# Hybrid encoder block on one core: compressed rows from the first token-major pass, first attention's values as a fifth seven-product group

## The reference, cut to what matters

```
h = rmsnorm(x); proj = h @ w_in                      # columns: AQ AK AV AG | CQ CKV KR BG | MG
oa = diff_attention(aq, ak, av)                      # 8 heads; ya = (rmsnorm(oa) * silu(ag)) @ w_oa
q  = rmsnorm(cq)  @ w_uq;  kv = rmsnorm(ckv) @ w_ukv # cq and ckv: 512 compressed columns each
ob = attention(q_nope|rope(q_rope), k_nope|rope(kr), vb);  yb = (ob * silu(bg)) @ w_ob
x  = x + (sigmoid(ga) * ya + sigmoid(gb) * yb) @ w_out;  out = rmsnorm(x)
```

## Time and profile before

| | us |
|---|---|
| Median of 3 runs (1456.37 to 1456.82) | 1456.66 |
| Profiled execution, its own time | 1456.54 |
| Its span in the profile | 1454.7 |
| PE busy | 1438.2 (99% of the span) |
| DVE busy | 982.3 (68%) |
| ACT busy | 653.6 (45%) |
| DMA, mean rate | 143 GB/s |

### The profile page before, as it was taken

The page is one execution under the profiler, slowest core; times in us unless marked ns, Lnnn a source line. Parts: engine busy times, 40 slices in busy tenths (PEclk is TensorE's granted clock), DMA queues, the critical chain, the costliest instruction groups (busy, mean ns, idle before and its releaser), DMA issues.

```text
span 1454.7 us, 18138 instructions
## 1 busy us (share of the span) xinstructions
PE 1438.2 (99%) x6780; PEld 1198.1 (82%) x6780; DVE 982.3 (68%) x1354; ACT 653.6 (45%) x835; POOL 44.6 (3%) x58
## 2 busy tenths in 40 slices
PE   8999999999999999999999999999999999999997
PEld 7888888888888888888888888888888888888886
DVE  6967798888777666666665643666667353578966
ACT  7534353434345455454543335565565122324434
POOL 0000000000000111001110000000000000000000
PEclk9999999999999999999999999999999999999999
DMA  8349585757562322322222334322332444616674
GB/s 300 137 153 309 157 276 174 259 183 225 186 191 83 83 78 77 89 79 79 79 72 73 97 91 145 87 74 58 93 127 70 150 125 145 202 59 228 194 249 182
DMA packets 189535, 207.94 MB, mean 143 GB/s; under 512 B 19360, under 2 KB 144416, under 8 KB 188832
## 3 DMA queue, kind: packets, MB, share of 16 engines
q1 hardware_dynamic: 181952, 189.25, 42.3%
q10 hardware_dynamic: 7520, 17.83, 3.1%
HBM read 187.12 MB, written 19.92 MB: 142 GB/s over the span
## 4 chain that ended last, share of the span: by engine, by line
PE 91%; DVE 4%; DMA 2%; SPq 1%; issue 1%; ACT 1%; POOL 0%; POOLq 0%; DVEq 0%
PE duo L2028 28%; PE duo L2030 27%; PE duo L2029 27%; PE duo L2081 2%; PE duo L2055 1%; PE duo L2058 1%; DMA start_y<-start_columns 1%; DVE m_lo L1422 1%; PE duo L2114 1%; SPq L598 1%; PE duo L2108 1%; PE duo L2077 1%; PE duo L2073 0%; PE duo L2076 0%; PE duo L2074 0%
## 5 line engine op out<-in xcount | busy, mean ns | idle before, releaser
L1310 DVE TENSOR_TENSOR w_lo<-w_raw,w_hi 128x1024 fp32r<-128x1024 f32 (+1 forms) x134 | 157.4, 1175 | 157.8 <-ACT w_hi L756 157.2
L2028 PE MATMUL duo<-h_hi,w_hi 128*128 128x512 f32 x656 | 260.2, 397 | 0.0
L2030 PE MATMUL duo<-h_hi,w_lo 128*128 128x512 f32 x656 | 255.9, 390 | 0.0
L2029 PE MATMUL duo<-h_lo,w_hi 128*128 128x512 f32 x656 | 255.7, 390 | 0.0
L756 ACT ACTIVATE w_hi<-w_raw 128x1024 fp32r<-128x1024 f32 (+1 forms) x134 | 136.2, 1017 | 173.9 <-DMA w_raw<-in_w_ob_dram 65.3
L857 ACT ACTIVATE m_hi<-m_raw 128x2048 fp32r<-128x2048 f32 (+1 forms) x56 | 98.0, 1753 | 118.8 <-PE duo L2030 47.7
L2030 PEld LDWEIGHTS duo<-h_hi,w_lo 128*128 128x128 f32 x656 | 123.1, 188 | 26.7
L2028 PEld LDWEIGHTS duo<-h_hi,w_hi 128*128 128x128 f32 x656 | 123.3, 188 | 23.9 <-DVE q_hl L1315 0.3
L2029 PEld LDWEIGHTS duo<-h_lo,w_hi 128*128 128x128 f32 x656 | 123.4, 188 | 23.7
L1422 DVE TENSOR_TENSOR m_lo<-m_raw,m_hi 128x2048 fp32r<-128x2048 f32 (+3 forms) x61 | 121.2, 1989 | 21.3 <-ACT m_hi L857 20.8
L2028 PE MATMUL duo<-m_hi,h_hi 128*128 128x512 f32 x320 | 126.0, 394 | 2.0 <-DVE h_lo L1458 1.0
(11 more groups left out here) (296 smaller groups left out, 2807.6 us busy)
## 6 DMA issues: line engine op xcount, KB each, us to landing
m_raw<-in_w_in_dram SPq DMA_DIRECT2D x94, 512.0 KB, 4.6
w_raw<-in_w_in_dram SPq DMA_DIRECT2D x164, 256.0 KB, 3.2
o_raw<-in_w_out_dram SPq DMA_DIRECT2D x32, 512.0 KB, 5.5
w_raw<-in_w_oa_dram SPq DMA_DIRECT2D x32, 256.0 KB, 3.4
sig<-gates SPq DMA_DIRECT2D x8, 1024.0 KB, 6.5
w_raw<-in_w_ob_dram SPq DMA_DIRECT2D x32, 256.0 KB, 3.4
spare<-in_w_in_dram SPq DMA_DIRECT2D x13, 512.0 KB, 4.4
h_raw<-in_w_in_dram SPq DMA_DIRECT2D x13, 512.0 KB, 5.1
```

Source lines behind the costliest of these rows:

```text
L1310: dve.tensor_tensor(w_lo[:, piece.slot, 0:cols], w_raw[:, piece.slot, 0:cols], w_hi[:, piece.slot, 0:cols].bitcast(F32), ALU.subtract).the ...
L2028: pe.matmul(dst, lhs_hi, rhs_hi, start=start, stop=False)
L2029: pe.matmul(dst, lhs_hi, rhs_lo, start=False, stop=False)
L2030: return pe.matmul(dst, lhs_lo, rhs_hi, start=False, stop=stop)
```

## The change

The first pass now reads CQ and CKV, whose rows come out token-major. ACT squares each row with an accumulator and scales it by its inverse root, and the rows are stored to `compressed`. AV becomes group 0 of five seven-product groups; its blocks are stored to `values` without a sigmoid. In the compressed stage the 16 pieces for CKV and CQ are gone; SP loads the stored rows back as `c_tok`, PE turns them with 8 x 4 transposes (`turn_c`) within the half pieces 2 to 11, ACT and DVE split them straight from PSUM with the gain. The first BG pair comes first, then KR, then `token_values`, one token tile at a time in two banks, head 7's extras 8 to 11 between its tiles. `rope_angles` moves to step 2, `rope_tables` to step 3, `rotate` to step 5. Three orders are changed: DVE makes the low part first also in the step after each group's first step and in one more step of the `w_out` group, and the first quarter of the gated rows is split one step earlier. Cut to its core:

```diff
-A_STEPS, C_STEPS, B_STEPS = 6, 24, 4
+A_STEPS, C_STEPS, B_STEPS = 6, 8, 4
+KR_STEP, VB_STEP = 2, 4
+C_TURN_AT = (2, 4, 5, 6, 8, 9, 10, 11)
+C_TURN_BANK = (1, 2, 3, 2, 3, 2, 3, 2)
-M_GROUPS, GROUP = 4, 1024
+M_GROUPS, GROUP = 5, 1024
-LOW_FIRST += [OUT0 + L_STEPS + i for i in range(3)] + [MID_SPLIT]
+LOW_FIRST += [end + 1 for end in SECOND_END[:M_GROUPS - 1]]
+LOW_FIRST += [OUT0 + L_STEPS + i for i in range(4)] + [MID_SPLIT]
+C_SQUARE_AT, C_SCALE_AT, C_VAR_AT = (8, 9, 14, 15), (12, 13, 17, 18), (10, 16)
...                                                   # SP
+            compressed_in(0)                         # 1 MB, ahead of the stage's pieces
+                    if g == 0 and half == 0:
+                        sp.wait_ge(max_taken, HEADS * TOK)
+                        sp.wait_ge(dist_halved, HEADS * TOK - 1)
+                        compressed_in(1)
...                                                   # ACT, first pass and group 0
+            def square_c(t): ...
+                    act.activation(post_z[...], c_rows[t][...], ACT.Square, accum_out=c_ss[:, i:i + 1])
+            def scale_c(t): ...
+                    act.activation(part, part, ACT.Copy, scale=c_rstd[...]).then_inc(c_scaled, 1)
+                act.dma_start(c_d[t * P:(t + 1) * P, :], c_rows[t][:, :]).then_inc(v_out[t // 2], 16)
...                                                   # ACT, compressed stage
+                for q in (2 * s, 2 * s + 1):
+                    if q >= 2 * VB_STEP:
+                        keep_vb(q - 2 * VB_STEP)
+                    if q in C_TURN_AT:
+                        c_hi_of(C_TURN_AT.index(q))
+                    if q == 2 * VB_STEP:
+                        act.wait_ge(used, C0 + KR_STEP + 2)
+                        rope_shift(0, ACC[1])
-                if s == 9:
+                if s == 3:
                     rope_tables()
-                if s == 19:
+                if s == 5:
                     rope_his(0)
...                                                   # ACT and DVE, last head of the second attention
-            quarter_hi(0)
+                if s == 0:
+                    quarter_hi(0)
...                                                   # DVE, compressed stage
+                for q in (2 * s, 2 * s + 1):
+                    if q in C_TURN_AT:
+                        c_lo_of(C_TURN_AT.index(q))
-                if s == 7:
+                if s == 2:
                     rope_angles()
+                if s == 5:
+                    rotate(0, ACC[1], acc_read)
...                                                   # PE, compressed stage
+            def turn_c(i):
+                j, k = i // LT, i % LT
+                pe.wait_ge(c_in[j], 16)
+                if i == 0:
+                    pe.wait_ge(acc_read, A_READ0)
+                elif i < 3:
+                    pe.wait_ge(max_taken, HEADS * TOK)
+                else:
+                    pe.wait_ge(c_lo_ready, i - 1)
+                for t in range(TOK):
+                    last = pe.transpose(bank[C_TURN_BANK[i]][:, t * P:(t + 1) * P], c_tok[:, j, t, k * P:(k + 1) * P], ident)
+            def tail(q):
+                if q < 2 * A_STEPS:
+                    a_extras(q, HEADS, False, True)
+                if q in C_TURN_AT:
+                    turn_c(C_TURN_AT.index(q))
+            def token_values(g):
+                for t in range(TOK):
+                    j = g * TOK + t
+                    if j == 0:
+                        pe.wait_ge(c_lo_ready, LT)
+                    if j >= 2:
+                        pe.wait_ge(v_kept, TOK + j - 1)
...
+                        last = three(SC[2 + j % 2][:, :], c_hi[:, kt, q], c_lo[:, kt, q], hi, lo, kt == 0, kt == LT - 1)
+                    tail(2 * VB_STEP + j)
+            for s in range(VB_STEP):
+                if s == KR_STEP:
+                    pe.wait_ge(c_lo_ready, 1)
+                project(Piece(C0 + s), ACC[s // 2], s % 2, 2, h_hi, h_lo, 8 * (s % 2), lambda: tail(2 * s))
+                tail(2 * s + 1)
+            for g in range(2):
+                token_values(g)
```

More of the change, by code:

```diff
@@ L373, in place_of @@
             return mg_place if g == OUT_G else h_place
+        c_d = nc.dram_tensor("compressed", (SEQ, 2 * LORA), F32, kind="Internal").ap()
         v_d = nc.dram_tensor("values", (SEQ, HEADS * P), F32, kind="Internal").ap()
@@ L722, in _ @@
                 rsqrt(x_rstd[:, t:t + 1], x_var[:, t:t + 1], x_var_ready, t + 1, x_rstd_ready)
+            for i in range(2):
+                rsqrt(c_rstd[:, 4 * i:4 * i + 4], c_var[:, 4 * i:4 * i + 4], c_var_ready, i + 1, c_rstd_ready)
             pool.wait_ge(m_used, N_MERGE)
@@ L2374, in _ @@
                     a_head(head, True)
-            def token_values(g, half):
-                piece = Piece(C0 + VB_STEP + 2 * g + half)
-                pe.wait_ge(lo_ready, piece.after(0))
-                if not half:
-                    pe.wait_ge(c_lo_ready, LT)
-                for i in range(TOK):
-                    t = (i + 2 * g) % TOK
-                    if not half and g == 0 and i == 0:
-                        pe.wait_ge(o_normed, HEADS)
-                    if not half and g:
-                        if i < 2:
-                            pe.wait_ge(v_kept, TOK + i + 1)
-                        if i == 2:
-                            pe.wait_ge(c_scaled, 2 * LT)
-                    q = slice(t * P, (t + 1) * P)
-                    for k in range(2):
-                        hi, lo = tile(piece, k * SEQ, SEQ)
-                        kt = 2 * half + k
-                        last = three(bank[VB_BANKS[g][t]][:, :], c_hi[:, kt, q], c_lo[:, kt, q], hi, lo,
-                                     kt == 0, kt == LT - 1)
-                    if half and i < TOK - 1:
-                        last.then_inc(v_full, 1)
-                last.then_inc(used, 1)
@@ new lines, in tail @@
+            def tail(q):
[4 more added lines that the diff above has]
+            def token_values(g):
+                pieces = [Piece(C0 + VB_STEP + 2 * g + half) for half in range(2)]
+                for t in range(TOK):
+                    j = g * TOK + t
+                    if j == 0:
+                        pe.wait_ge(c_lo_ready, LT)
+                        pe.wait_ge(max_taken, HEADS * TOK)
+                    if j >= 2:
+                        pe.wait_ge(v_kept, TOK + j - 1)
+                    q = slice(t * P, (t + 1) * P)
+                    for kt in range(LT):
+                        if t == 0 and kt % 2 == 0:
+                            pe.wait_ge(lo_ready, pieces[kt // 2].after(0))
+                        hi, lo = tile(pieces[kt // 2], kt % 2 * SEQ, SEQ)
+                        last = three(SC[2 + j % 2][:, :], c_hi[:, kt, q], c_lo[:, kt, q], hi, lo, kt == 0, kt == LT - 1)
+                        if t == TOK - 1 and kt % 2:
+                            last.then_inc(used, 1)
+                    if t < TOK - 1:
+                        last.then_inc(v_full, 1)
+                    tail(2 * VB_STEP + j)
```

256 lines of the change are left out of this document (106 added, 150 removed).

## The result

The changed kernel takes 1462.61 us (median of five runs, 1461.72 to 1464.93) against 1456.59 (1456.24 to 1456.82) for the kernel before on the same chip: ratio 1.0044, 95% interval 1.0033 to 1.0056. It is slower by 6.0 us; the forecast was no change, 1456.4, and the time lies above the forecast's range. Its profiled execution took 1462.61 us with a span of 1460.8, 6.1 more than before's 1454.7.

The account below looks back on a forecast made before the run. PE, busy 1438.2 of 1454.7 us, was taken as the bound. 48 saved matmuls (10.9 us) against new waits 8.1, added group's borders 0.9 and low-part orders 1.8 gave -0.1 from 1456.54: 1456.4 us, range 1450.0 to 1460.8.

Parts of the forecast that it names:

- Steps 1 to 4: Compressed stage: pieces removed -87.0 us, column sums and spreads removed -3.6, transposes added +3.5; seven-product group added +77.1.
- the rival by which they cost their full duration: Compressed stage: 32 transposes cost 10.6 us instead of 3.5, time 1463.5; chance 0.03.
- Steps 5 to 7: PE waits, compressed stage: A before KR 3.6 us, B before head 7's last values product 3.7, C before tile 6 0.8.
- The rival without A and B: Compressed stage: the waits ahead of KR and head 7's last values product are absent, time 1449.1; chance 0.20.
- Step 8: Sum of the compressed stage: -79.0 us, so 63 us instead of 142.
- Step 9: Groups' borders, low part first: PE's wait moves one step on and grows, +0.4 us per border, +1.6 for four.
- Step 10: Low part first in the `w_out` group: a wait of 0.69 goes, DVE is later afterwards; +0.2 us.
- Step 11: Quarter's split made earlier: wait of 1.51 us before the Y product goes, 1.0 comes at the values product; net -0.6.
- Step 12: Stores of the compressed rows: `sum_w` waits for the last store's landing; +0.6 us, from 0 to 3.4.
- Step 13: Put at nothing: ACT's squares and scalings, four sigmoids fewer, and SP's two loads of 1 MB.
- three signs of being wrong: Compressed stage 56 us or less, fifth group over 79 us, or PE waiting on `v_kept` at more than one tile.
- The slower rival (ACT bounds the eight token tiles): Compressed stage: tiles wait for ACT's keep two tiles back, +4.0 us on five other tiles, time 1460.4; chance 0.24.

Follow-up runs that it names:

- experiments 5: Changed kernel with 15 unused matmuls put ahead of KR and 15 ahead of head 7's last values product; faster than the changed kernel by 1.7 us.
- experiment 12: Kernel before with the low part ahead of the first Y product made three times instead of once; 1461.58 us, +4.5.
- experiment 11: Kernel before with only the low part first also at the second step after each group's end; 1458.41 us, ratio 1.0011.
- experiment 1: Changed kernel with DVE's rotary angles one step later, tables in step 4 in place of 3; 1459.24 us.
- experiment 2: Changed kernel with the turned blocks in the two score banks only; 1457.93 us.
- (6): Changed kernel with the second four values tiles made by halves in four banks and kept at the stage's last step; 1462.57 us.

## Why the prediction was wrong

The mechanisms that it named were there, and nearly all sizes were right; it failed by what it left out. By its steps:

- **Steps 1 to 4** (matmuls, sums, transposes, group): right. 6732 matmuls on the page are its count; the four transposes take the pace of the earlier trace rows, so the rival by which they cost their full duration (1463.5) is out, though its time is near the one measured.
- **Steps 5 to 7** (waits A, B, C): right. Forecast 3.6, 3.7 and 0.8, in the trace 3.56, 3.69 and 0.67. The rival without A and B is out.
- **Step 8, the sum of the stage, is the step that failed.** It added the waits to the matmuls at 0.2267 and made 63 us; the trace has 66.6. It took for granted that PE comes out of a wait of 3.6 us at the pace at which it went in. It doesn't: two stretches at half clock cost 3.2 us, and experiments 5 and 12 show that PE's standing still is the cause. Without them the time would be 1459.4 by subtraction, inside the range. The kernel before has no wait in this size behind the first matmuls, so no row of it showed this, and behind the longest, 1.51 us, the pace was the usual one.
- **Step 9** (borders): right mechanism, the wait one step on; 0.52 and not 0.4 each, 2.1 for 1.6. Its bound of a gain "excluded above 0.15" held (experiment 11).
- **Step 10** (+0.2): +0.1 in the trace. **Step 11** (-0.6): the wait is at the values product with 0.86, forecast 1.0; with the new wait on `gated` (1.2 us from start to start) taken out of the +0.6, the net is -0.6.
- **Step 12** (+0.6): +0.6 in that execution, but the landing varies from one execution to the next, and in experiment 1 a wait of 1.94 there brought the clock down too. That the middle fit was luck. The two rows it took (5.7 and 7.8) were not all that the kernel before has: the other stores of 512 KB to `values` landed after 2.7, 3.1 and 7.1 us.
- **Step 13** put the loads at nothing. It checked the load that stands behind the 1 MB transfer in SP's queue, not when a slot comes free: +1.2 us on `gated`.
- **Not named at all:** the tail, +0.8 us.

Clock 3.2, `gated` 1.2, tail 0.8, borders 0.5, and 0.4 elsewhere up to the A-heads, whose cause stays open, make 6.1 us; the measured difference is 6.1 where the sum had -0.1. What is left of the stage (+0.3) and of the A-heads and steps 10 and 11 (-0.3) cancels. None of the prediction's three signs of being wrong came up: the stage is over 56 us, the fifth group under 79 (77.6), and one tile waits. None of them looked at the pace of the matmuls. The slower rival (ACT bounds the eight token tiles) did not happen: PE waits on `vb_keep` at one tile.

## What to carry to other kernels

Price a wait of PE of several us at more than its length, here 10.9 us for two waits of 7.25 together, and look at the granted clock within and behind it, since the busy share counts the slow matmuls as work. The extra isn't a fixed sum: the same wait B cost 1.7 us more in one profile and 2.6 in another. Before you move a product into a bank or a small engine's work into a queue, ask who reads that bank and what PE wants next from that queue: two edits of a few lines gave back 9.6 us. Ask also when each slot comes free after the order of the loops has changed, not only when its load stands in the queue.

## What the runs showed of the hardware that was not expected

Where the clock falls, within a wait or behind it, differs for one and the same wait. In the changed kernel the first start at the slow pace is 0.9 us behind the end of wait A. In experiment 1, at the same wait of 3.56 us, and at the 4.03 us of experiment 12, the clock was down before PE resumed: the first matmul took 0.79 and 0.76 us, not 0.50 as in the changed kernel. What came late by it ranges from 1.4 us (wait A in experiment 1) to 2.6 (wait B in experiment 2). Waits of 3.56, 3.69, 4.03 and once 1.94 us were followed by it; waits of 1.51 (before), 1.61 (experiment 1), 1.70 (6) and 1.37 (5) were not. Fifteen matmuls whose result nobody wants, put into each of two such waits, made the kernel faster by 1.7 us.

The tail is 0.8 us longer in each profile in which a packet of instructions runs among the last stores, and 32 more instructions in DVE's program moved the packet away (8.0 against 8.8 us). In a kernel measured to 0.1%, that is something which an edit elsewhere can bring or take.
